# The weight products of a unit by row tile and term with the token chunks innermost, in a two-layer hybrid decoder step on one core

## What is computed

```python
u = rmsnorm(x, a_norm) @ a_w_in            # 1024 x 2048: gate and xb
xc = causal_dwconv(xb)                     # width 4
r = sigmoid(blockwise(xc, gate_r_w)); i = sigmoid(blockwise(xc, gate_i_w))
hs = lru_scan(exp(log_a(r)), sqrt(1 - a * a) * (i * xc), h0)
x = x + (gelu(gate) * hs) @ a_w_out
x = x + conv_ffn(rmsnorm(x))               # g, v = xn @ w_up; (gelu(conv(g)) * v) @ w_down
k, v = split(rmsnorm(x) @ w_kv + b_kv)
q = qnorm(rmsnorm(x) @ w_q + b_q)
x = x + swa(q, k, v, sinks, rel_bias) @ w_o + b_o
x = x + conv_ffn(rmsnorm(x))
```

## Time and profile before

| | us |
|---|---|
| median of 3 runs | 2708.9 (2707.06 to 2710.8) |
| span of the profiled execution | 2706.0 |
| TensorE busy in it | 2569.1 |
| VectorE, ScalarE, GpSimd busy in it | 1288.9, 877.0, 282.7 |

### The profile page before, as it was taken

How to read it: one execution, slowest core, us unless ns; L and a number is a source line. 1 busy time by engine, 2 the same in 40 slices (tenths; PEclk the granted TensorE clock), 3 DMA queues, 4 the chain that set the end, 5 groups by cost and what they waited for, 6 DMA issues and landing times.

```text
span 2706.0 us, 39679 instructions
## 1 busy us (share of the span) xinstructions
PE 2569.1 (95%) x15074; PEld 2452.0 (91%) x15074; DVE 1288.9 (48%) x1803; ACT 877.0 (32%) x1559; POOL 282.7 (10%) x386
## 2 busy tenths in 40 slices
PE   5999888999999999999899799899999999999998
PEld 4999887999999999999789455698999999999998
DVE  7566546432342333343766889436333333333432
ACT  3554523421331331222443455324313312311211
POOL 2011233000000000002320133221000000000000
PEclk7999889999999999999999889999999999999999
DMA  3111110111111111111251300011111111111112
GB/s 108 40 40 39 39 39 25 54 37 49 47 39 47 47 41 45 47 43 43 46 78 32 118 1 1 16 39 39 43 43 48 43 41 54 39 41 53 39 43 81
DMA packets 220401, 121.96 MB, mean 45 GB/s; under 512 B 22429, under 2 KB 217949, under 8 KB 220220
## 3 DMA queue, kind: packets, MB, share of 16 engines
q1 hardware_dynamic: 218068, 117.19, 14.8%
q10 hardware_dynamic: 2196, 3.74, 1.2%
q0 software_dynamic: 64, 0.05, 0.0%
HBM read 112.31 MB, written 10.55 MB: 45 GB/s over the span
## 4 chain that ended last, share of the span: by engine, by line
PE 79%; DVE 12%; issue 4%; ACT 3%; DMA 2%; POOL 1%; SPq 0%; ACTq 0%; DVEq 0%; POOLq 0%
PE ps L640 25%; PE ps L642 25%; PE ps L641 25%; DVE stat L1761 1%; DMA raw<-in_w_q 1%; PE ps L910 1%; DVE stat L1748 1%; DVE rstd L1409 1%; DVE nlo L1440 1%; DVE convin L1432 1%; DVE y L1432 1%; DVE pb L1739 1%; PE ps L952 1%; DVE wlo L1404 1%; PE ps L813 0%
## 5 line engine op out<-in xcount | busy, mean ns | idle before, releaser
L640 PE MATMUL ps<-nhi,whi 128*128 128x384 f32 (+1 forms) x3312 | 1096.0, 331 | 65.9 <-POOL nlo L1858 26.8
L642 PE MATMUL ps<-nhi,wlo 128*128 128x384 f32 (+1 forms) x3312 | 1086.2, 328 | 0.0
L641 PE MATMUL ps<-nlo,whi 128*128 128x384 f32 (+1 forms) x3312 | 1085.7, 328 | 0.0
L640 PEld LDWEIGHTS ps<-nhi,whi 128*128 128x128 f32 x3312 | 626.5, 189 | 85.2 <-issue 70.7
L641 PEld LDWEIGHTS ps<-nlo,whi 128*128 128x128 f32 x3312 | 627.0, 189 | 1.6 <-issue 0.2
L642 PEld LDWEIGHTS ps<-nhi,wlo 128*128 128x128 f32 x3312 | 626.4, 189 | 0.0
L1404 DVE TENSOR_TENSOR wlo<-raw,whi 128x1024 fp32r<-128x1024 f32 (+2 forms) x220 | 244.9, 1114 | 623.4 <-ACT whi L1019 623.3
L642 PE MATMUL ps<-hhi,wlo 128*128 128x384 f32 (+1 forms) x1152 | 375.9, 326 | 0.0
L640 PE MATMUL ps<-hhi,whi 128*128 128x384 f32 (+1 forms) x1152 | 375.8, 326 | 0.0
L641 PE MATMUL ps<-hlo,whi 128*128 128x384 f32 (+1 forms) x1152 | 375.6, 326 | 0.0
L1019 ACT ACTIVATE whi<-raw 128x1024 fp32r<-128x1024 f32 (+2 forms) x220 | 208.3, 947 | 448.9 <-PE ps L642 439.7
(11 more groups left out here) (242 smaller groups left out, 2188.3 us busy)
## 6 DMA issues: line engine op xcount, KB each, us to landing
raw<-in_f_w_up SPq DMA_DIRECT2D x96, 512.0 KB, 3.8
raw<-in_f_w_down SPq DMA_DIRECT2D x64, 384.0 KB, 3.5
raw<-in_a_w_in SPq DMA_DIRECT2D x16, 512.0 KB, 4.0
xrows<-in_x_prompt SPq DMA_DIRECT2D x8, 512.0 KB, 6.5
raw<-in_a_w_out SPq DMA_DIRECT2D x8, 512.0 KB, 4.1
raw<-in_w_q SPq DMA_DIRECT2D x16, 256.0 KB, 3.7
raw<-in_w_o SPq DMA_DIRECT2D x32, 128.0 KB, 2.9
strip<-strip_sb ACTq DMA_DIRECT2D x1, 3072.0 KB, 33.9
```

Source lines behind the costliest of these rows:

```text
L640: pe.matmul(out, whi[s][:, w], mhi[:, k, chunk(c)], start=(k == 0), stop=False)
L641: pe.matmul(out, whi[s][:, w], mlo[:, k, chunk(c)], start=False, stop=False)
L642: last = pe.matmul(out, wlo[s][:, w], mhi[:, k, chunk(c)], start=False, stop=(k == nk - 1))
```

## The change

A new function `rotate` takes the place of three `piece` calls in every unit that has neither `before` nor `stats_of`. It waits for the slot's three banks at its start. Then, for each row tile k and each of the three terms, it issues three products with the same weights, one for each chunk, into three banks. `bank_ready` of the three banks is counted up at the last three products of the unit.

```diff
+            def rotate(n, s, nk, mhi, mlo):
+
+                for c in range(3):
+                    wait(pe, bank_free[3 * s + c], n)
+                for k in range(nk):
+                    w = ds(k * P, P)
+                    for wt, mv, first, final in ((whi, mhi, True, False), (whi, mlo, False, False), (wlo, mhi, False, True)):
+                        for c in range(3):
+                            last = pe.matmul(bank(3 * s + c, c), wt[s][:, w], mv[:, k, chunk(c)],
+                                             start=(first and k == 0), stop=(final and k == nk - 1))
+                            if final and k == nk - 1:
+                                last.then_inc(bank_ready[3 * s + c], 1)
...
                 pe.wait_ge(hi_ready[s], n + 1)
                 pe.wait_ge(lo_ready[s], n + 1)
+                if before is None and stats_of is None:
+                    rotate(n, s, nk, mhi, mlo)
+                    return
```

## The result

The changed kernel takes 2734.65 us (median, 2732.7 to 2737.33) beside 2707.98 for the kernel before in the same job: a ratio of 1.009 (95% interval 1.0071 to 1.0109), slower by about 26 us. The forecast was 2714. The time lies in the range that I gave and the sign was the likelier one, but that is luck as far as my sum goes: it had 5 us of loss, all in the readers, and the range reached up to this time only for the low end of rival (a). The step "The products themselves: no change" failed.

A forecast was written before the change was run, and what follows sets the result against it. Bound: the distance between product starts on TensorE in feed-forward blocks, ScalarE and VectorE in part of each recurrent pass. Span 2706.0 + 4.9 for the readers + 2.9 to the runs' median gave 2713.8, given as 2714; range 2706 to 2740.

The forecast's parts named there:

- the readers: Three banks ready together make reads about 1 us later; TensorE's waits in the recurrent block grow, 4.9 us in all.
- rival (a): Each change of width costs at the array: 15 us or more, 2729, up to 2822; chance 0.24, mostly low end.
- The products themselves: no change: On TensorE, the same products with the same columns keep their distances; weights, banks and widths add or save nothing.
- the third step of the products, the width: Width now changes at every third product and back; taken as zero, with ends of +108 and -36 us.
- The bounds: Per change of width: 0.03 us extra at a unit's opening from above, nothing or 0.01 us gained from below.
- weights and banks: Three products in a row on the same weights drop no load, and going to three banks neither gains nor loses.
- rival (e): Rotating banks lets TensorE's clock fall; a tenth of the products at the lower level would cost 151 us; chance 0.02.
- passes 0 to 3: Recurrent block's delays: 0.87 us in pass 0, 1.05 each in passes 1 and 2, 1.92 in pass 3.
- its two terms: Pass 3 of the recurrent block: 0.87 us for two gelus before one split, 1.05 for two sigmoids before the next.
- the count of the units: The forecast took 31 units of 54 products to rotate, with 10,818 products in 3,606 groups in all.
- rival (c): Read bursts meet a queue at the 8 starts of the down products: up to 8 us more, 2722; chance 0.05.
- nothing is lost at the end: After the last unit two more additions end near 2686.5, while TensorE waits for a state copy until 2689.11: no cost.

The follow-up runs named there:

- snake: The changed kernel with the chunks of every second group in the order 2, 1, 0: 2748.33 us, 1.0137 of the kernel before.
- equal_new: The changed kernel with chunks of 364, 364 and 360 tokens in place of 384, 384 and 320: 2740.55 us, 1.0115 of the kernel before.
- equal_old: The kernel before with chunks of 364, 364 and 360 tokens in place of 384, 384 and 320: 2735.18 us, ratio 1.0092.
- late_ready: The changed kernel with the old chunk-by-chunk order of products, all three banks still becoming ready together at the unit's end: 2716.35 us, 1.0019 of the kernel before.
- wide_last: The changed kernel with chunks of 352, 352 and 384 tokens in place of 384, 384 and 320: 2715.48 us, 1.0010 of the kernel before.
- c368_new: The changed kernel with chunks of 368, 368 and 352 tokens in place of 384, 384 and 320: 2725.77 us, 1.0064 of the kernel before.
- wide_last_old: The kernel before with chunks of 352, 352 and 384 tokens in place of 384, 384 and 320: 2720.46 us, ratio 1.0033.
- c368_old: The kernel before with chunks of 368, 368 and 352 tokens in place of 384, 384 and 320: 2713.66 us, ratio 1.0012.
- kc: The changed kernel with the chunk loop between row tile and term, so three products of one chunk in a row: 2735.35 us, 1.0094 of the kernel before.

## Why the prediction was right or wrong

**Wrong: the third step of the products, the width.** The text says "I take zero, since a price of columns plus a constant describes both widths inside their stretches". It does, inside the stretches: the rotating order has none. The bounds held the truth, 6.7 ns a group between +30 and -10, and the row that told of it was the unit's opening, the only place in the kernel before where a narrow product is followed by a wide one. I had explained the opening away with the unit's waits. The starts of the rows above would have told: a wait delays one product, and here the second to the fifth are late, with none of them waiting for anything. Rival (a) had the right place and, in its "0.003 to 0.023 by the rounding", the size; it should have been the forecast. A fixed price for each change, as its first words have it, is out too: snake has half of the changes and loses more. From 6.7 ns come, outside of the recurrent block: a 72-product unit pays 24 x 6.7 = 161 ns, less the 20 that it paid once before, 141 ns; a 54-product unit 18 x 6.7 - 20 = 101 ns. 109 x 0.141 + 33 x 0.101 = 18.7 us of the 26.1.

**Right: weights and banks.** The Trainium skill's page "TensorE: Matmul & The Clock Gate" ("Part 2: What happens when you issue a matmul") has one load serve many products. Here the loads stay one for each product, and equal_new against equal_old shows that three products on the same weights gain nothing. The same page's section "A second HAM failure mode: psum-queue depth-cycling" has a rotation of banks let the clock swing; no row shows it, the clock is 1.00 over 810 us with a new bank at every product of the changed units. That was rival (e).

**Right in sum, less so in its parts: the readers.** ScalarE after the last gate unit of the first pass, in the changed kernel:

```profile
187.91 1.05 ACT L1149 ACTIVATE z<-ps,pcol 128x384 f32 x2 [0.49 <-PE ps L653]
188.86 1.06 ACT L1035 ACTIVATE whi<-raw 128x1024 fp32r<-128x1024 f32 x1
```

Both sigmoids now stand between the unit's end and the split, as said, 0.95 us by the starts (predicted 1.05, against the earlier trace rows). In late_ready, where only this is changed, the two rows read the same at 186.89 and 187.83. TensorE's waits behind the chain, the answers to the earlier trace rows:

```profile
215.91 0.66 PE L653 MATMUL ps<-nhi,whi 128*128 128x384 f32 x1 [3.32 <-issue]
...
321.17 1.25 PE L653 MATMUL ps<-xchi,whi 128*128 128x384 f32 x3 [6.59 <-DVE wlo L1420]
...
357.43 0.69 PE L771 MATMUL ps<-nhi,whi 128*128 128x384 f32 x1 [10.21 <-DVE nlo L1618]
```

The output projection resumes 4.5 us later (the prediction called this its start); 4.9 were predicted. By passes (from one start of unit 4c + 1 to the next) passes 0 to 3 take 0.79, 1.37, 1.30 and 1.01 us more, where 0.87, 1.05, 1.05 and 1.92 were predicted. In late_ready passes 1 to 3 take 1.23, 1.13 and 0.97 more. So a pass costs somewhat more than the two sigmoids in the middle passes, and pass 3 about half of its two terms. There the gate units begin at the lower clock: behind the wait to 317.07 the kernel before runs 13 products at 320 or 267 ns, after runs 11, which is 0.3 of the missing 0.9 us. The rest I didn't separate. Nor are the waits 1 us longer each, as I had written: those to 213.71 and 317.07 read 3.42 and 6.26 us before and 3.32 and 6.59 now. The period grew, and most of its growth lies elsewhere in the pass.

**Missed: the norm sums at the end of layer 0's feed-forward block.** The last down unit of slot 0 rotates, and all three of its chunks come at once to be added to `x` on VectorE (L1620, L1636 after), squared on ScalarE (L1169, L1185 after) and summed on GpSimd (L1851, L1867 after). TensorE's sums in the next unit wait for that unit's first chunk to go the same way. Before:

```profile
1294.85 1.04 ACT L1019 ACTIVATE whi<-raw 128x1024 fp32r<-128x1024 f32 x1
...
1297.09 0.56 DVE L1620 TENSOR_TENSOR x<-ps,x 128x384 f32<-128x384 f32 x1
...
1298.80 0.34 PE L642 MATMUL ps<-hhi,wlo 128*128 128x384 f32 x1
1299.35 0.91 PE L664 MATMUL ps<-t,ones 128*128 128x384 f32 x2 [0.21 <-POOL t L1851]
```

and after:

```profile
1310.08 1.04 ACT L1035 ACTIVATE whi<-raw 128x1024 fp32r<-128x1024 f32 x1
...
1312.50 0.54 DVE L1636 TENSOR_TENSOR x<-ps,x 128x384 f32<-128x384 f32 x1
...
1313.40 0.34 PE L642 MATMUL ps<-hhi,wlo 128*128 128x384 f32 x1
1314.72 0.91 PE L680 MATMUL ps<-t,ones 128*128 128x384 f32 x2 [0.98 <-POOL t L1867]
```

with GpSimd ahead of it:

```profile
1309.51 3.80 POOL L1867 TENSOR_TENSOR t<-t,t 128x384 f32<-128x384 f32 x3 [5.09 <-ACT t L1185]
1313.68 0.99 POOL L1867 TENSOR_TENSOR t<-t,t 128x384 f32<-128x384 f32 x1 [0.37 <-ACT t L1185]
```

The distance of the two products grows from 0.55 to 1.32 us, and in late_ready it is 1.34: 0.8 us for the burst. GpSimd isn't what holds it up: its three sums end at 1313.31, and the next waits 0.37 us for the square. The delay comes down the other two engines. ScalarE squares three chunks ahead of its split, VectorE's split follows that one, and only then comes the addition that the square needs. Counted from the unit's first product (1293.74 before, 1308.35 after), ScalarE's split starts 0.6 us later and the addition 0.8 us later. I had cleared the feed-forward blocks with slot 0's copies being needed a unit later, and hadn't looked at this unit, whose readers feed the norm. It is the same oversight as in the count of the units.

**Right: no wait at the down products, rival (c).** TensorE runs through the start of the down products, and VectorE's first `hlo` begins at 600.14:

```profile
598.37 0.66 PE L653 MATMUL ps<-nhi,wlo 128*128 128x384 f32 x3
598.87 0.34 PE L640 MATMUL ps<-hhi,whi 128*128 128x384 f32 x1
...
600.14 1.42 DVE L1675 TENSOR_TENSOR hlo<-y,hhi 128x384 fp32r<-128x384 f32 x3
```

**Right: nothing is lost at the end.** After the last product TensorE waits as in the earlier trace rows, before transposes that start 26.1 us later, like the last products:

```profile
2710.88 1.04 PE L818 MATMUL ps<-ident,fstash 128*18 128x128 f32 x8
...
2715.20 3.06 PE L1016 MATMUL ps<-ident,x 128*128 128x128 f32 x26 [0.68 <-ACT fout L1236]
```

**The sum.** 18.7 for the width outside of the recurrent block, 4.5 in it for all causes, 0.8 for the sums are 24.0 of the 26.1 us. Of the rest, 1.4 arise between the sums of squares at 1299.35 and the statistics at 1341.46 (1314.72 and 1358.24 after), where the clock's mean is 0.88 instead of 0.96 (1314 to 1358 us in after, 1298 to 1341 in before).

**What stays open.** That the widths in turn cost the 6.7 ns is shown, by wide_last and equal_new; the rule behind it isn't: what makes the second to fifth wide product late, why some returns from 352 columns are free, and why c368_new pays 1.7 ns a group over its own old order where wide_last pays none. Why wide_last_old takes more than the kernel before. No version was faster than the kernel before; late_ready shows that even a rotating order whose products cost nothing extra has some 5 us to win back, since it makes all of a unit's banks ready at once.

## What to carry to other kernels

An order of loops that mixes sizes creates transitions which the old stream has only at its seams: look at the seam's own rows, product by product, over the six that follow, before calling the extra there a wait. They show that there is a price; its size in the new order they gave here only roughly. A bank that is ready after a third of a unit is worth something wherever its reader is behind, so the innermost loop over chunks has to be paid for with something, and in these runs reused weights paid nothing. Where TensorE is always busy, count its products in a fixed stretch; the busy time doesn't move.

## What the runs showed of the hardware

- In a stream at 2.4 GHz the starts of these products are 173.3 ns apart for 384 columns and 146.7 for 320, (columns + 32) / 2.4 GHz. Other widths keep to it less well: 352 columns take 159.7 on average in wide_last_old and 158.3 in c368_old (160.0 by the formula), 368 take 167.9 in c368_old (166.7). 364 and 360 columns take 166.3 and 166.6 in equal_old, about what 368 would, but 360 took 163.3 in the down units of equal_new. At the lower clock the distances are 320 ns and 267 ns, with nothing on top.
- After a return to a wider product, the first six distances at 384 columns are 175, 177, 185, 176, 182, 173 ns, at all 76 unit openings of the 810 us in the kernel before and in the midst of a unit in kc. After 352 columns (wide_last_old) 46 of 76 returns read so and 30, those of down units, read 174, 175, 173, 174, 173, 173.
- Three products in a row on the same weights have three loads in the trace and take as long as with three different weights; three banks in turn cost nothing.
